# Opening of a one-core encoder kernel: decay series behind the up weights, x loaded in other pieces, the second gate half later, twelve products of ones instead of fifteen

## The reference, cut to what matters

```python
def rmsnorm(x, g):
    r = lax.rsqrt(jnp.mean(x32 * x32, axis=-1, keepdims=True) + EPS)
    return (x32 * r * g)
def swiglu(h, w_gate, w_up, w_down):
    return (jax.nn.silu(h @ w_gate) * (h @ w_up)) @ w_down
# first thing that reference() does in a layer
x = x + 0.5 * swiglu(rmsnorm(x, norm_ffn1[l]), ffn1_gate[l], ffn1_up[l], ffn1_down[l])
# two small tables that do not depend on x
log_gamma = jnp.log1p(-jnp.exp2(-decay_exp))      # (2, 4) per layer, for the retention's decay
bias = rel_bias[bucket]                           # relative bias of the dilated attention
```

## Time and profile before

| quantity | value |
|---|---|
| median of 3 runs (lowest, highest) | 2587.11 us (2587.04, 2587.2) |
| the profiled execution's own time | 2586.7 us |
| its span, first to last instruction | 2584.9 us |
| TensorE busy | 2571.9 us, 99% |
| VectorE busy | 1902.2 us, 74% |
| ScalarE busy | 1164.3 us, 45% |
| mean granted TensorE clock | 1.000 |

### The profile page before, as it was taken

The page is one execution under the profiler, slowest core; times in us unless marked ns, Lnnn a source line. Parts: engine busy times, 40 slices in busy tenths (PEclk is TensorE's granted clock), DMA queues, the critical chain, the costliest instruction groups (busy, mean ns, idle before and its releaser), DMA issues.

```text
span 2584.9 us, 38836 instructions
## 1 busy us (share of the span) xinstructions
PE 2571.9 (99%) x14769; PEld 2281.2 (88%) x14769; DVE 1902.2 (74%) x2374; ACT 1164.3 (45%) x1787; POOL 77.7 (3%) x79
## 2 busy tenths in 40 slices
PE   9999999999999999999999999999999999999999
PEld 7999997888888888999989999878888888889998
DVE  8877879777775469777788778796776844697776
ACT  5433446556563234433443334565655622443332
POOL 1111001000000000000000000010000000000000
PEclk9999999999999999999999999999999999999999
DMA  5433242332343333333223232432433433333331
GB/s 186 148 123 116 66 156 89 103 113 90 104 151 112 96 111 122 99 104 98 98 82 123 97 97 74 145 98 89 126 90 90 156 118 98 114 115 98 100 108 54
DMA packets 231231, 281.50 MB, mean 109 GB/s; under 512 B 14645, under 2 KB 185058, under 8 KB 230830
## 3 DMA queue, kind: packets, MB, share of 16 engines
q1 hardware_dynamic: 225960, 270.63, 33.0%
q0 software_dynamic: 4512, 5.04, 0.7%
q10 hardware_dynamic: 646, 4.31, 0.4%
HBM read 265.52 MB, written 19.04 MB: 110 GB/s over the span
## 4 chain that ended last, share of the span: by engine, by line
issue 55%; PE 43%; POOL 1%; DVE 0%; DMA 0%; ACT 0%; POOLq 0%; ACTq 0%
PE proj L663 11%; PE proj L665 11%; PE proj L664 11%; PE acc L663 3%; PE acc L664 3%; PE acc L665 3%; PE acc L1017 0%; POOL y_hi L650 0%; POOL work L652 0%; PE acc L944 0%; DVE ring_lo L1947 0%; PE acc L965 0%; PE acc L927 0%; PE acc L928 0%; POOL y_lo L654 0%
## 5 line engine op out<-in xcount | busy, mean ns | idle before, releaser
L663 PE MATMUL proj<-h_hi,ring_hi 128*128 128x256 f32 (+1 forms) x1632 | 548.1, 336 | 1.3 <-DVE h_lo L1904 1.3
L665 PE MATMUL proj<-h_hi,ring_lo 128*128 128x256 f32 (+1 forms) x1632 | 544.0, 333 | 0.0
L664 PE MATMUL proj<-h_lo,ring_hi 128*128 128x256 f32 (+1 forms) x1632 | 543.7, 333 | 0.0
L663 PE MATMUL proj<-y_hi,ring_hi 128*128 128x256 f32 (+1 forms) x1504 | 463.6, 308 | 0.0
L665 PE MATMUL proj<-y_hi,ring_lo 128*128 128x256 f32 (+1 forms) x1504 | 463.0, 308 | 0.0
L664 PE MATMUL proj<-y_lo,ring_hi 128*128 128x256 f32 (+1 forms) x1504 | 462.9, 308 | 0.0
L1348 ACT ACTIVATE ring_hi<-raw 128x1024 fp32r<-128x1024 f32 (+1 forms) x175 | 210.1, 1204 | 360.3 <-PE acc L665 194.6
L663 PEld LDWEIGHTS proj<-h_hi,ring_hi 128*128 128x128 f32 x1632 | 310.1, 190 | 33.1 <-DVE ring_lo L2671 1.7
L665 PEld LDWEIGHTS proj<-h_hi,ring_lo 128*128 128x128 f32 x1632 | 310.0, 190 | 30.5
L664 PEld LDWEIGHTS proj<-h_lo,ring_hi 128*128 128x128 f32 x1632 | 310.1, 190 | 28.8
L665 PEld LDWEIGHTS proj<-y_hi,ring_lo 128*128 128x128 f32 x1504 | 287.3, 191 | 13.8
(11 more groups left out here) (299 smaller groups left out, 4198.1 us busy)
## 6 DMA issues: line engine op xcount, KB each, us to landing
raw<-in_ffn_gate SPq DMA_DIRECT2D x88, 512.0 KB, 3.6
raw<-in_ffn_up SPq DMA_DIRECT2D x88, 512.0 KB, 4.2
raw<-in_w_in SPq DMA_DIRECT2D x136, 256.0 KB, 3.6
raw<-in_w_in SPq DMA_DIRECT2D x60, 512.0 KB, 5.2
raw<-in_ffn_down SPq DMA_DIRECT2D x56, 512.0 KB, 4.3
work<-in_ffn_down SPq DMA_DIRECT2D x32, 512.0 KB, 5.8
raw<-in_w_out SPq DMA_DIRECT2D x16, 512.0 KB, 4.3
raw<-in_w_ret_o SPq DMA_DIRECT2D x12, 512.0 KB, 4.0
```

Source lines behind the costliest of these rows:

```text
L663: pe.matmul(o, s_hi, m_hi, start=start, stop=False, skip_group_check=onto)
L664: pe.matmul(o, s_hi, m_lo, start=False, stop=False, skip_group_check=onto)
L665: return pe.matmul(o, s_lo, m_hi, start=False, stop=stop, skip_group_check=onto)
```

## The change: what it does

The eight tiles of x are loaded as tile 0, tile 1, tiles 2 to 4 and tiles 5 to 7, and the second gate half is issued ahead of the last of these instead of after the first pair. ScalarE and VectorE take up the second gate half ahead of tile 3 instead of tile 2. ScalarE's three decay instructions move behind its copy of the up weights. VectorE's `decay_series` moves from the start to behind its subtraction of the up weights, and `decay_logs` from ahead of that subtraction to behind the move of the first bias bank. Twelve products of ones stand where fifteen stood.

```diff
--- before.py
+++ after.py
@@ -80,7 +80,8 @@
 FIRST_CREDIT = 9
 FREE = 1
 LO_CREDIT = 2
-WARM, EARLY_SQUARES = 15, 3
+WARM, EARLY_SQUARES = 12, 3
+X_PARTS = ((0, 1), (1, 2), (2, 5), (5, 8))
 FIRST_COLS = ((C_RV, 2, RET_DV), (C_DQ, 1, P))
 FIRST_WIDTH = 3 * P
 FIRST_PARTS = ((0, 5), (5, 8))
@@ -547,10 +548,10 @@
 
 
             gate_up(0, 0, 0, 0, 0)
-            for c in range(4):
-                if c == 1:
+            for c, (k0, k1) in enumerate(X_PARTS):
+                if c == 3:
                     gate_up(0, 0, 0, 1, 0)
-                sp.dma_start(xs[:, 2 * c:2 * c + 2, :], x.rearrange("(k p) n -> p k n", p=P)[:, 2 * c:2 * c + 2, :]).then_inc(x_in[c], 16)
+                sp.dma_start(xs[:, k0:k1, :], x.rearrange("(k p) n -> p k n", p=P)[:, k0:k1, :]).then_inc(x_in[c], 16)
             sp.dma_start(relb[0:N_BUCKETS, :], rel_bias).then_inc(bias_in, 16)
             sp.dma_start(work[0:N_BUCKETS + 1, 8:12, :], c_onehot[:, 0:2048].rearrange("p (t n) -> p t n", n=512)).then_inc(bias_in, 16)
             sp.dma_start(onehot[4][:, 0:256], c_onehot[:, 2048:2304]).then_inc(bias_in, 16)
@@ -1839,26 +1840,28 @@
             act.dma_start(d_e[:, :], decay_rows).then_inc(decay_in, 16)
             act.dma_start(params[:, :], rows_t).then_inc(params_in, 16)
             act.dma_start(ident[:, :], c_ident).then_inc(ident_in, 16)
+            act.wait_ge(ffn_landed[0][0], 16)
+            act.activation(ring_hi[:, 0:PIECE], raw[:, 0, 0:PIECE], ACT.Copy).then_inc(first_hi, 1)
+            act.wait_ge(params_in, 16)
+            for m in range(KT):
+                if m == 3:
+                    act.wait_ge(ffn_landed[0][1], 16)
+                    act.activation(ring_hi[:, PIECE:2048], raw[:, 0, PIECE:2048], ACT.Copy).then_inc(weights_hi, 1)
+                for c, (k0, k1) in enumerate(X_PARTS):
+                    if m == k0:
+                        act.wait_ge(x_in[c], 16)
+                gained_hi(0, m)
+            for m in range(EARLY_SQUARES):
+                square(m)
+            act.wait_ge(ffn_landed[1][0], 16)
+            act.wait_ge(ffn_landed[1][1], 16)
+            act.activation(ring_hi[:, 2 * PIECE:4 * PIECE], raw[:, 1, :], ACT.Copy).then_inc(weights_hi, 1)
             act.wait_ge(decay_in, 16)
             act.activation(d_y[:, :], d_e[:, :], ACT.Exp, scale=-math.log(2.0)).then_inc(d_exp, 1)
             act.wait_ge(d_exp, 1)
             act.activation(d_w[:, :], d_y[:, :], ACT.Copy, scale=-1.0, bias=1.0).then_inc(d_exp, 1)
             act.wait_ge(d_exp, 2)
             act.activation(d_ln[:, :], d_w[:, :], ACT.Ln).then_inc(d_log, 1)
-            act.wait_ge(ffn_landed[0][0], 16)
-            act.activation(ring_hi[:, 0:PIECE], raw[:, 0, 0:PIECE], ACT.Copy).then_inc(first_hi, 1)
-            act.wait_ge(params_in, 16)
-            for m in range(KT):
-                if m == 2:
-                    act.wait_ge(ffn_landed[0][1], 16)
-                    act.activation(ring_hi[:, PIECE:2048], raw[:, 0, PIECE:2048], ACT.Copy).then_inc(weights_hi, 1)
-                act.wait_ge(x_in[m // 2], 16)
-                gained_hi(0, m)
-            for m in range(EARLY_SQUARES):
-                square(m)
-            act.wait_ge(ffn_landed[1][0], 16)
-            act.wait_ge(ffn_landed[1][1], 16)
-            act.activation(ring_hi[:, 2 * PIECE:4 * PIECE], raw[:, 1, :], ACT.Copy).then_inc(weights_hi, 1)
             for m in range(EARLY_SQUARES, KT):
                 square(m)
             for c in range(1, 5):
@@ -2152,8 +2155,10 @@
 
                 if N == 0:
                     lo(1, 2, 2048, raw[:, 1, :])
+                    decay_series()
                     dve.wait_ge(bias_mm, 1)
                     dve.tensor_copy(bdiag[0], bias_banks[0][0:12, :]).then_inc(bias_first, 1)
+                    decay_logs()
                     add_squares(N)
                 else:
                     add_squares(N)
@@ -2666,17 +2671,15 @@
                     w = min(512, NT * WD - 512 * c)
                     dve.tensor_copy(sel_r[:, 512 * c:512 * c + w], onehot[c][:, 0:w]).then_inc(sel_ready, 1)
 
-            decay_series()
             dve.wait_ge(first_hi, 1)
             dve.tensor_tensor(ring_lo[:, 0:PIECE], raw[:, 0, 0:PIECE], ring_hi[:, 0:PIECE].bitcast(fp32), ALU.subtract).then_inc(first_lo, 1)
             for m in range(KT):
-                if m == 2:
+                if m == 3:
                     dve.wait_ge(weights_hi, 1)
                     dve.tensor_tensor(ring_lo[:, PIECE:2048], raw[:, 0, PIECE:2048], ring_hi[:, PIECE:2048].bitcast(fp32),
                                       ALU.subtract).then_inc(weights_lo, 1)
                 gained_lo(0, m)
             bias_operands()
-            decay_logs()
             for l in range(DEPTH):
                 ffn(l, 0, 3 * l + 1)
                 heads(l, 0, False, 3 * l + 1)
```

## The result

| | before | changed |
|---|---|---|
| median of 20 runs | 2586.93 us | 2591.28 us |
| lowest | 2586.11 | 2590.22 |
| highest but strays | 2588.51 | 2593.0 |
| profiled execution: own time / span | 2586.7 / 2584.9 | 2590.67 / 2588.8 |

The ratio of the times is 1.0018, 95% interval [1.0011, 1.0024]: slower by 4.35 us, which is within the 0.2% that I had called no change. The median is 0.4 us above the forecast of 2590.9. The loss itself was forecast as 3.8 us, so it is 0.55 us larger than that. One time of the kernel before is a stray (5091 us); it is counted in the median, which is 2586.83 without it.

The account below looks back on a forecast made before the run. TensorE was taken as the bound, busy 2571.9 of 2584.9 us. Terms -1.3 (start), +1.1 (tile 3), +2.3 (`bias_first`), +1.7 (squares) sum to 3.8 us: 2590.9 us from the median 2587.11, range 2588.6 to 2593.0.

Parts of the forecast that it names:

- Start: Opening: with the decay instructions gone from ahead, TensorE's first real product starts at 8.14, 1.29 us earlier.
- 1.9 us at most: Opening: the largest gain at the start, should `params` come as early as ScalarE's copy is done.
- Tile 3: TensorE waits 1.0 to 1.3 us for the later second gate half; tile 3 begins at 13.2 to 13.5.
- Series ahead of the bank: VectorE's series stands ahead of its move of the first bias bank: `up` starts at 24.8, 2.1 us later.
- Logs ahead of the squares: Six more VectorE instructions ahead of the squares: TensorE can sum at 30.7, 3.8 us later than before.
- TensorE between `up` and the sums: From `up` at 24.8 TensorE reaches the sums by itself at 29.0, then waits 1.7 us more.
- three signs of being wrong: `up` before 24, line-719 matmuls before 30, or products behind the waits over 0.6 us long.
- The clock rival: TensorE's clock falls in the new wait, costing some 2.0 us; 2592.9 if it stands whole; chance 10%.
- Nothing is won back behind it: Behind line 718 both engines start from the same event, so distances between them stay as before.
- the rival of an absorbed delay: Later waits, the two for GpSimd of 3.2 us in sum, absorb the delay; 0.6 remains, 2587.7; chance 6%.
- The up weights land later: VectorE's chain starts from their landing, one for one; a landing 1 us later gives 2591.9; chance 5%.
- Twelve for fifteen: Start of TensorE's list: three products of ones fewer cost and give nothing, ending before x was there in both kernels.

Follow-up runs that it names:

- Experiment 3: decay_alone: kernel before with only the decay instructions of ScalarE and VectorE moved; x loads, gate half and fifteen products of ones as before; 2590.98 us, ratio 1.0017.
- experiment 2: x_fifteen: kernel before with only x's new pieces and the later second gate half, fifteen products of ones kept, decay unmoved; 2586.60 us, ratio 0.9999.
- Experiment 4: bank_first: changed kernel with VectorE's move of the first bias bank ahead of the series; series and logs then precede the squares; 2593.43 us, ratio 1.0025.
- experiment 8: fill_wait: changed kernel with nine more products of ones between the bias table and `up`; 2591.55 us, ratio 1.0020.
- x_alone: Experiment 1: kernel before with only x's new pieces, the later second gate half and twelve products of ones; decay unmoved; 2587.98 us, 2587.53 without a stray.
- logs_behind: Changed kernel with the six instructions of the logs moved behind the addition of the squares; 2591.42 us, ratio 1.0018.
- bank_fill: The kernel of bank_first with seventeen products of ones added ahead of the sums of squares; 2592.28 us, ratio 1.0020.
- spread: Changed kernel with Exp and Copy early, Ln behind the second tile, series split, logs behind the squares, second gate half ahead of tile 4; 2586.50 us, ratio 1.0000.

## Why the prediction was right, step by step

- **Start, -1.3 forecast.** It was 1.70 us (7.73). `params` landed at 1.46 + 4.1 = 5.6 instead of 6.47, and then VectorE's subtraction of the gate weights (5.69 to 6.92) was what the first low part waited for, a bound that my "1.9 us at most" had left out. As forecast, nearly all of the gain was gone by tile 3.
- **Tile 3, 1.1 us, begins at 13.2 to 13.5.** Measured 1.09, at 13.22. The line drawn through the bytes of the queue was good to 0.2 us. Tile 3 of the kernel before was at 13.62 and not at the 13.5 that I worked out, which changed nothing.
- **Series ahead of the bank, `up` at 24.8.** Measured 24.64. The series took 23.86 - 20.83 = 3.03 us there, as at its old place. Experiment 3 has the loss from the decay alone, experiment 2 has none from x.
- **Logs ahead of the squares, squares ready for 30.7, 3.8 us later.** Measured 30.38 for the squares and 30.44 for the sums, 3.55 later. Experiment 4 shows that this chain decides and the wait for the bank doesn't: taking that wait away made the kernel slower. The mechanism was right, and overlaps and a chain that began 0.08 us sooner took the rest.
- **TensorE between `up` and the sums: wrong, and covered by luck.** I let it take 4.2 us with the clock at its upper level and then wait 1.7 us. It took 5.80 us at the lower level and did not wait. One of my three signs of being wrong, products of over 0.6 us behind the waits, did come true. The number held because the fall cost 1.6 us and the wait that would have stood there was 1.5 us long (1.47 in experiment 8).
- **The clock rival, 10%.** I had the chance of a fall too low: every trace with an unfilled wait of over 2 us ahead of `up` or of the sums has one. What the rival said of the cover was right: fallen in the first wait it is nearly covered, standing alone it is paid. Its price of 2.0 us was a middle value that no trace shows: 1.5 to 1.6 us in the changed kernel, x_alone and logs_behind, 2.5 in decay_alone (6.74 instead of 4.20 us from `up` to the sums) and 3.2 in bank_first (6.93 us from the sums to line 725, against 3.77 in bank_fill).
- **Nothing is won back behind it.** The offset is 3.55 us at the sums, 3.66 at the end of the opening, 3.98 at the first wait for GpSimd and 3.9 at the end of the span. The two waits for GpSimd are still 1.6 us each, so the rival of an absorbed delay fell. The 0.3 us between the second and the third of these belong to single executions rather than to the change: fill_wait has 3.71 and 3.41 there.
- **The up weights land later, 5%.** Not in the changed kernel's profile (ScalarE took them up at 16.67, before at 16.74). But the moment moved between 16.57 (x_fifteen) and 17.46 (logs_behind) over the traces. The kernel before has 0.85 us to spare at the sums (squares ready at 26.04, sums at 26.89) and can hide much of that; the changed one has nothing to spare. That fits its wider spread and the 0.55 us above the forecast loss, but no run tests it.
- **Twelve for fifteen.** "Cost and give nothing" was right for the whole change and wrong as a general statement: it rests on the earlier start (experiments 1 and 2).
- **How the profile would show it.** I expected the wait at `up` to be put down to VectorE's move. It stands as "issue".

The measured median is 0.4 us above the forecast. The times of the changed kernel spread over 2.8 us, those of the kernel before mostly over 1.3. What makes the upper ones stays open: filling the wait did not remove them.

## What to carry to other kernels

Before moving a chain of small dependent instructions to where "the engine has time", look for the first instruction behind it in that engine's list that another engine waits for: 16 instructions of 0.16 us stood ahead of one copy that released the bank and put it off by 2.7 us (21.18 to 23.86). The engine that bounds the kernel had 0.8 us to spare there (copy done at 21.86, `up` at 22.69), and lost all the rest. An early start is worth only what the next fixed point leaves of it (here 1.7 us at the start, 0.4 at tile 3, nothing at `up`), so find that point first. And removing a wait ahead of a longer one gives nothing, or loses where the merged wait lets the clock fall with no cover behind it.

## What the runs showed of the hardware that I had not expected

- The granted clock fell with idle times of 2.13, 2.80, 2.95 and 4.14 us, and in one profiled execution of x_alone with 1.89 us, but not with the 1.6 us waits for GpSimd. The moment differs: inside the wait in decay_alone (23.3), as TensorE resumed in logs_behind and bank_first, 0.7 us after that in x_alone, 1.4 us after it in the changed kernel. It was low for 3.4 us in the changed kernel, x_alone and logs_behind, and for 6.8 us in decay_alone and bank_first.
- x_alone's two groups of times suggest that the same program falls in some executions and not in others; only one execution of each kernel has a trace. For the rise at the start of a kernel, the Trainium skill (TensorE: Matmul & The Clock Gate, What's actually happening) says that the number of slow products varies between runs of the same kernel. The traces agree with that: the twelve products of ones at the beginning took 4.32 us in the changed kernel's profile and 5.49 us in spread's.
- Nine or seventeen more matmuls at the beginning of TensorE's list brought a wait put down to issue at one far place (about 2060 us), 0.5 us with nine, 0.9 or 1.5 with seventeen. Its position in the program was the same in all four kernels, and without added matmuls logs_behind lost 0.2 us there. So an experiment that adds instructions has to be compared at a milestone of the trace near the edit as well, not by its total time alone.
